# Modulation weights in pieces of two K-tiles by 1024 columns, scale ahead of shift by halves, three input blocks begun on the first half of the K-tiles

## The reference, cut to what matters

```python
def ada_modulation(cvec, w_mod, b_mod):            # w_mod: 2048 x 12288
    m = jax.nn.silu(cvec) @ w_mod + b_mod
    return jnp.split(m[:, None, :], N_MOD, axis=-1)

sh1, sc1, g1, sh2, sc2, g2 = ada_modulation(cvec, lp['w_mod'], lp['b_mod'])
h = rmsnorm(x, lp['n1']) * (1.0 + sc1) + sh1
... = split_columns(h @ lp['w_in'])
```

## Time and profile before

| | |
|---|---|
| median of 3 runs | 2429.8 us (2429.21 to 2432.45) |
| profiled execution, its own time | 2430.1 us |
| its span in the trace | 2428.3 us |
| TensorE busy | 2204.9 us (91%) |
| first matmul with w_in | 144.92 us |
| first matmul behind the mixed stage (L711) | 642.54 us |
| `w_mod` loads | 96 of 1024 KB |

### The profile page before, as it was taken

The page is one execution under the profiler, slowest core; times in us unless marked ns, Lnnn a source line. Parts: engine busy times, 40 slices in busy tenths (PEclk is TensorE's granted clock), DMA queues, the critical chain, the costliest instruction groups (busy, mean ns, idle before and its releaser), DMA issues.

```text
span 2428.3 us, 44041 instructions
## 1 busy us (share of the span) xinstructions
PE 2204.9 (91%) x19325; PEld 1948.0 (80%) x19325; DVE 1142.7 (47%) x2079; ACT 773.5 (32%) x1300; POOL 94.9 (4%) x140
## 2 busy tenths in 40 slices
PE   3789999999777888886997999999999999999997
PEld 1268888888545666665997999999999999887885
DVE  1122223544495787874346444444444444445445
ACT  2122222222253434342334332333333333333432
POOL 1000000000301111110000000000000000000000
PEclk8579999999876999998998999999999999999998
DMA  8977777777701001004325334334334435333341
GB/s 293 348 254 233 231 225 243 245 224 226 179 2 28 7 3 33 3 5 171 109 87 174 122 128 133 122 123 137 122 122 132 129 122 180 132 122 121 121 133 59
DMA packets 283472, 338.78 MB, mean 140 GB/s; under 512 B 9502, under 2 KB 268180, under 8 KB 281425
## 3 DMA queue, kind: packets, MB, share of 16 engines
q1 hardware_dynamic: 281440, 329.77, 42.2%
q0 software_dynamic: 1840, 6.20, 1.0%
HBM read 328.43 MB, written 10.28 MB: 139 GB/s over the span
## 4 chain that ended last, share of the span: by engine, by line
PE 80%; DVE 11%; DMA 4%; ACT 2%; issue 2%; POOL 0%; DVEq 0%; SPq 0%; POOLq 0%; ACTq 0%
PE ps L616 23%; PE ps L618 22%; PE ps L617 22%; DMA ring<-in_w_mod_dram 3%; PE ps L654 3%; PE ps L663 1%; PE ps L808 1%; PE ps L802 1%; PE ps L798 1%; DVE arena L1681 1%; PE ps L979 1%; DMA arena<-in_x_sample_dram 1%; DVE stat L1542 1%; DVE w_split L1386 1%; PE ps L818 1%
## 5 line engine op out<-in xcount | busy, mean ns | idle before, releaser
L1386 DVE TENSOR_TENSOR w_split<-ring,w_split 128x1024 fp32r<-128x1024 f32 (+1 forms) x392 | 475.7, 1219 | 760.2 <-ACT w_split L1086 759.9
L1086 ACT ACTIVATE w_split<-ring 128x1024 fp32r<-128x1024 f32 (+1 forms) x392 | 407.4, 1052 | 736.1 <-PE ps L618 592.1
L616 PE MATMUL ps<-h_split,w_split 128*128 128x384 f32 x1776 | 598.2, 337 | 11.8 <-DVE w_split L1386 8.5
L618 PE MATMUL ps<-h_split,w_split 128*128 128x384 f32 x1776 | 594.9, 335 | 0.0
L617 PE MATMUL ps<-h_split,w_split 128*128 128x384 f32 x1776 | 594.9, 335 | 0.0
L616 PEld LDWEIGHTS ps<-h_split,w_split 128*128 128x128 f32 x1776 | 334.7, 188 | 23.8 <-issue 12.0
L617 PEld LDWEIGHTS ps<-h_split,w_split 128*128 128x128 f32 x1776 | 334.6, 188 | 0.0
L618 PEld LDWEIGHTS ps<-h_split,w_split 128*128 128x128 f32 x1776 | 334.5, 188 | 0.0
L616 PE MATMUL ps<-w_split,h_split 128*128 128x256 f32 x960 | 275.2, 287 | 12.6 <-DVE w_split L1386 12.6
L617 PE MATMUL ps<-w_split,h_split 128*128 128x256 f32 x960 | 272.2, 284 | 0.0
L618 PE MATMUL ps<-w_split,h_split 128*128 128x256 f32 x960 | 272.1, 283 | 0.0
(11 more groups left out here) (362 smaller groups left out, 2732.4 us busy)
## 6 DMA issues: line engine op xcount, KB each, us to landing
ring<-in_w_mod_dram SPq DMA_DIRECT2D x96, 1024.0 KB, 8.2
ring<-in_w_up_dram SPq DMA_DIRECT2D x88, 1024.0 KB, 5.1
ring<-in_w_in_dram SPq DMA_DIRECT2D x46, 1024.0 KB, 6.9
ring<-in_w_down_dram SPq DMA_DIRECT2D x44, 1024.0 KB, 5.3
ring<-in_w_out_dram SPq DMA_DIRECT2D x16, 1024.0 KB, 5.8
arena<-in_x_sample_dram SPq DMA_DIRECT2D x4, 1024.0 KB, 12.8
x_mid<-arena SPq DMA_DIRECT2D x1, 3072.0 KB, 10.2
h_f<-x_mid SPq DMA_DIRECT2D x1, 3072.0 KB, 9.9
```

What stands on the lines that cost most here:

```text
L616: mm(o_, lh, rh, start=start, stop=False)
L618: return mm(o_, ll, rh, start=False, stop=stop)
L1086: AC(wh[k % SPLITS][:, 0:width(n)], arrived(n), ACT.Copy).then_inc(s_hi, 1)
L1386: V.tensor_tensor(wl[k % SPLITS][:, 0:w], arrived(n), wh[k % SPLITS][:, 0:w].bitcast(F32), ALU.subtract).then_inc(s_lo, 1)
```

## The change

`w_mod` comes in pieces of two K-tiles by 1024 columns (rows of 4 KB); a block is 1024 columns, so there are 12 blocks of 8 pieces and not 48 of two. A part is one K-tile; its four matmuls of 256 columns have the same stationary tile and go to the four groups of PSUM rows, which now hold four groups of columns; `mod_cols` spreads them with eight columns of the identity. The order is scale of K-tiles 0 to 7, shift of K-tiles 0 to 7, scale and shift of 8 to 15. Three pieces of `w_in` (the first half of the K-tiles of its blocks 0, 1 and 2) are moved into the second half of the front: the stream begins with 21 modulation pieces (0 to 20), then w_in (21), six modulation pieces, w_in (28), five modulation pieces, w_in (34), w_in block 0's second half (35), and 64 modulation and 44 more w_in pieces mixed. x is loaded after the first four pieces. The transposes of x move behind part 21 (the end of piece 10), the sigmoid of c ahead of the squares, and one tensor_reduce for expb goes. `h_mod` multiplies a half of the K-tiles at once; the shift is added in `h_hi` (four activations for a pair, in place of one) and `h_lo` (four in place of one).

```diff
@@ -59,7 +59,11 @@
-N_MOD = 6 * D // BLK
+MG = 4
+MOD_W = MG * BLK
+MOD_KP = PIECE // MOD_W
+MP = KT // MOD_KP
+N_MOD = 6 * D // MOD_W
...
@@ -69,27 +73,30 @@
-N_EARLY = 2 * D // BLK
-MOD_ORDER = [8 * (i % 2) + i // 2 for i in range(N_EARLY)] + list(range(N_EARLY, N_MOD))
-MIXED = [("mod", N_EARLY, 0), ("mod", N_EARLY, 1)]
-_left = [("mod", i, p) for i in range(N_EARLY + 1, N_MOD) for p in range(2)]
-_in = [("in", j, p) for j in range(len(IN_BLOCKS)) for p in range(2)]
+N_EARLY = 2 * D // MOD_W
+MOD_ORDER = [2, 0, 3, 1] + list(range(N_EARLY, N_MOD))
+EARLY_IN = 3
+STREAM = [("mod", i, p) for i in range(2) for p in range(MP)]
+for _p in range(2 * MP):
+    STREAM.append(("mod", 2 + _p // MP, _p % MP))
+    if _p in (4, 10, 15):
+        STREAM.append(("in", (4, 10, 15).index(_p), 0))
+_left = [("mod", i, p) for i in range(N_EARLY, N_MOD) for p in range(MP)]
+_in = [("in", j, 1) for j in range(EARLY_IN)] + [("in", j, p) for j in range(EARLY_IN, len(IN_BLOCKS)) for p in range(2)]
 for _i, _piece in enumerate(_in):
-    MIXED.append(_piece)
-    MIXED += _left[_i * len(_left) // len(_in):(_i + 1) * len(_left) // len(_in)]
-STREAM = [("mod", i, p) for i in range(N_EARLY) for p in range(2)] + MIXED
+    STREAM.append(_piece)
+    STREAM += _left[_i * len(_left) // len(_in):(_i + 1) * len(_left) // len(_in)]
...
@@ -106,12 +113,9 @@
+FRONT = MOD_END[3] + SPLITS
+H_AT = {MOD_END[1] + SPLITS - 1: (0, 1, 2, 3)}
+H_AT.update((MOD_END[3] + k, (4 + k,)) for k in range(4))
...
@@ -435,11 +443,13 @@
-            for t, src in ((0, a["x_prompt"][0]), (1, a["x_sample"][0, 0:P]), (2, a["x_sample"][0, P:2 * P])):
-                sp.dma_start(x[:, t, :], src).then_inc(s_x, 16)
             for n, (kind, i, p) in enumerate(STREAM):
+                if n == RING:
+                    for t, src in ((0, a["x_prompt"][0]), (1, a["x_sample"][0, 0:P]), (2, a["x_sample"][0, P:2 * P])):
+                        sp.dma_start(x[:, t, :], src).then_inc(s_x, 16)
                 if kind == "mod":
-                    load_piece(n, a["w_mod"][0], BLK * MOD_ORDER[i], BLK, p)
+                    src = a["w_mod"][0][MOD_KP * P * p:MOD_KP * P * (p + 1), MOD_W * MOD_ORDER[i]:MOD_W * (MOD_ORDER[i] + 1)]
+                    load(n, src.rearrange("(k p) c -> p k c", p=P), MOD_KP)
...
@@ -640,27 +650,21 @@
             def mod_part(n, i, p):
-                if n % 2 == 0 and p == 0 and i >= 2:
-                    if i - 2 < N_EARLY:
-                        pe.wait_ge(s_mrow, i - 1)
-                    else:
-                        pe.wait_ge(s_mcol, i - 1)
+                q = MOD_KP * p + n % 2
+                if q == 0 and i >= 2:
+                    pe.wait_ge(s_mcol, i - 1)
                 pe.wait_ge(s_w[n // 2 % RING], 16 * (n // 2 // RING + 1))
-                w_raw = arrived(n).rearrange("p (k c) -> p k c", k=KQ)
-                for k in range(KQ):
-                    q = KP * p + KQ * (n % 2) + k
-                    last = mm(ps[32 * k:32 * k + 2, i % 2, 0:BLK], c2_t[:, 2 * q:2 * q + 2], w_raw[:, k, :], start=(q == k), stop=(q == KT - KQ + k))
+                w_raw = arrived(n).rearrange("p (g c) -> p g c", g=MG)
+                for g in range(MG):
+                    last = mm(ps[32 * g:32 * g + 2, i % 2, 0:BLK], c2_t[:, 2 * q:2 * q + 2], w_raw[:, g, :], start=(q == 0), stop=(q == KT - 1))
                 last.then_inc(s_blk, 1)

             def mod_cols(i):
                 pe.wait_ge(s_mrow, i + 1)
...
                 for j in range(2):
-                    last = mm(ps[:, bank, at + 2 * j:at + 2 * j + 2], modrow[:, i % 2, toks(j)], expb[:, 9:11], start=True, stop=True)
+                    last = mm(ps[:, i % 2, BLK + 2 * MG * j:BLK + 2 * MG * (j + 1)], modrow(i)[:, toks(j)],
+                              ident.rearrange("p (g b) -> p g b", g=MG)[:, :, 0:2], start=True, stop=True)
...
@@ -699,7 +701,13 @@
-                if n - 3 in MOD_LAST:
+                if n == MOD_END[0] + 5:
+                    mod_cols(0)
+                    for t in range(3):
+                        turn_x(t)
+                if n in (MOD_END[1] - 1, MOD_END[2] + 1, MOD_END[3] - 1):
+                    mod_cols(1 + (n > MOD_END[1]) + (n > MOD_END[2] + 1))
+                if n - 3 in MOD_LAST and MOD_LAST[n - 3] >= N_EARLY:
                     mod_cols(MOD_LAST[n - 3])
...
@@ -1086,38 +1094,39 @@
+            def h_hi(j):
+                ac.wait_ge(s_mcol, 2 if j < PAIRS // 2 else 4)
+                ac.wait_ge(s_hm, j + 1)
+                for k in (2 * j, 2 * j + 1):
+                    for g, cols in ((0, slice(0, P)), (1, slice(P, TOK))):
+                        last = AC(hh[:, k, cols], xT[:, k, cols], ACT.Identity, bias=modcol[:, k, g:g + 1])
+                last.then_inc(s_hh, 1)
+
+            ac.wait_ge(s_vt, 1)
+            AC(csig, ps[:, 0, 0:2 * KT], ACT.Sigmoid).then_inc(s_csig, 1)
             for t in range(3):
                 ac.wait_ge(s_x, 48)
                 AC(junk, x[:, t, :], ACT.Square, accum_out=stat[:, t:t + 1]).then_inc(s_ssq, 1)
                 ac.wait_ge(s_ssq, t + 1)
-            ac.wait_ge(s_vt, 1)
-            AC(csig, ps[:, 0, 0:2 * KT], ACT.Sigmoid).then_inc(s_csig, 1)
+            mod_row(0)
...
-                AC(hh[:, 2 * j:2 * j + 2, :], xT[:, 2 * j:2 * j + 2, :], ACT.Copy).then_inc(s_hh, 1)
...
@@ -1419,45 +1427,58 @@
+            def h_mod(half_):
+                ks = slice(KT // 2 * half_, KT // 2 * (half_ + 1))
+                dv.wait_ge(s_mcol, 2 * half_ + 1)
+                link(V.scalar_tensor_tensor(scol[:, ks, :], modcol[:, KT:2 * KT, :][:, ks, :], 1.0, n1[:, ks, :], ALU.add, ALU.mult))
+                dv.wait_ge(s_xc, 12)
+                for k in range(ks.start, ks.stop):
+                    for g, cols in ((0, slice(0, P)), (1, slice(P, TOK))):
+                        last = V.tensor_scalar(xT[:, k, cols], xT[:, k, cols], scol[:, k, g:g + 1], None, ALU.mult)
...
+            def h_lo(j):
+                dv.wait_ge(s_mcol, 2 if j < PAIRS // 2 else 4)
+                dv.wait_ge(s_hm, j + 1)
+                dv.wait_ge(s_hh, j + 1)
                 for k in (2 * j, 2 * j + 1):
...
+                    for g, cols in ((0, slice(0, P)), (1, slice(P, TOK))):
+                        last = V.scalar_tensor_tensor(hl[:, k, cols], xT[:, k, cols], modcol[:, k, g:g + 1],
+                                                      hh[:, k, cols].bitcast(F32), ALU.add, ALU.subtract)
+                last.then_inc(s_h, 1)
...
+            for n in range(FRONT):
+                if n == MOD_END[0]:
+                    mod_col(0)
+                    h_mod(0)
+                if n == MOD_END[1]:
+                    mod_col(1)
+                if n == MOD_END[2] + 2:
+                    mod_col(2)
+                    h_mod(1)
+                if n == MOD_END[3]:
+                    mod_col(3)
...
```

More of the change, by code:

```diff
@@ L86 @@
 DOWN_W = PIECE // DOWN_KT
-MOD_LAST = {2 * n + 1: i for n, (kind, i, p) in enumerate(STREAM) if kind == "mod" and p == 1}
+MOD_LAST = {2 * n + 1: i for n, (kind, i, p) in enumerate(STREAM) if kind == "mod" and p == MP - 1}
 IN_LAST = {2 * n + 1: i for n, (kind, i, p) in enumerate(STREAM) if kind == "in" and p == 1}
@@ L91 @@
 MOD_END = {i: n + 1 for n, i in MOD_LAST.items()}
-PAIRS = N_EARLY // 2
+PAIRS = KT // 2
 SPLIT = [n for n in range(P_OUT) if STREAM[n // 2][0] == "in"]
@@ L258, in build @@
         crstd, o = carve(arena, o, CW)
-        modrow, _ = carve(arena, o, 2, BLK)
+        modrow2, _ = carve(arena, o, 2, BLK)
+        modrow1, _ = carve(ubuf, 0, 2, BLK)
         knew, o = carve(arena, o, 768)
@@ L413, in used, with modrow @@
                 eng.wait_ge(s_kd, n - P_DOWN + 1)
+        def modrow(i):
+            return (modrow1 if i < N_EARLY else modrow2)[:, i % 2, :]
         block = ctx.enter_context(nc.Block())
@@ L630, in _, with turn_x @@
                 tr(ps[:, g, 0:rows], vrow[0:rows, g, :], ident[0:rows, 0:rows]).then_inc(s_vt, 1)
-            for t in range(3):
+            def turn_x(t):
                 pe.wait_ge(s_xn, t + 1)
@@ L658, in mod_cols @@
                 pe.wait_ge(s_mrow, i + 1)
-                if i >= 2:
-                    pe.wait_ge(s_mcol, i - 1)
-                bank, at = (2 + i % 2, 0) if i < N_EARLY else (i % 2, BLK)
                 for j in range(2):
-                    last = mm(ps[:, bank, at + 2 * j:at + 2 * j + 2], modrow[:, i % 2, toks(j)], expb[:, 9:11], start=True, stop=True)
+                    last = mm(ps[:, i % 2, BLK + 2 * MG * j:BLK + 2 * MG * (j + 1)], modrow(i)[:, toks(j)],
+                              ident.rearrange("p (g b) -> p g b", g=MG)[:, :, 0:2], start=True, stop=True)
                 last.then_inc(s_mcT, 1)
@@ L670, in in_part @@
                 if n % 2 == 0 and p == 0:
-                    if j == 0:
-                        pe.wait_ge(s_mcol, N_EARLY)
                     for s in range(tiles):
@@ L1086, in hi, with mod_row @@
                 AC(wh[k % SPLITS][:, 0:width(n)], arrived(n), ACT.Copy).then_inc(s_hi, 1)
```

(48 more changed lines are left out.)

1 line of the change is left out of this document (removed).

## The result

The changed kernel takes 2392.85 us (median of 4 runs, 2391.87 to 2393.49) against 2431.03 for the kernel before beside it; the ratio is 0.9842 (95% interval 0.9829 to 0.9854). The profiled execution took 2392.75 us, its span is 2390.9. The forecast was 2389.

What follows compares the result with a forecast made beforehand. DMA engines were taken to bound the front until 144.92 us, PE the mixed stage after it. Front 13.8 us gained and mixed stage -26.8, together -40.6 on 2430.1, gave 2389 us; range 2373 to 2408.

Steps and rivals of the forecast that it cites:

- Start: Front: PE enters the modulation parts at about 20 us, 17 earlier, while the DMA doesn't stop.
- Rate: Front: 4 KB rows at 410 GB/s, 2.56 us a modulation piece; 28 pieces after x save 12.6 us.
- first rival: Front: 4 KB rows bring nothing, rate stays 348 GB/s, pieces take 3.01 us; 2397 us in all; chance 0.22.
- 372 GB/s: Front: estimate from the skill's fixed 3 cycles per packet, 2.82 us a modulation piece, about 2393 us in all.
- The transposes: Front: 48 transposes of x behind piece 10 keep PE longer than the ring lasts; 4.8 us lost.
- 8 us for the table: Front: the padded bias table, 2.7 MB within the DRAM, costs 8 us at 348 GB/s, as before.
- The w_in pieces: Front: early w_in pieces 21 and 28 hold PE longer than the ring lasts; 5.8 us lost, twice.
- second rival: Front: clock stays at half through the early w_in pieces, each stall grows by 6.5 us; 2408 us; chance 0.12.
- the third: Front: no stalls, hidden by pieces left in the ring and a clock already up; 2373 us; chance 0.10.
- Mixed stage: PE-bound stage: two w_in halves fewer -16.6, two modulation pieces more +1.8, fewer mod_cols -12.0; sum -26.8 us.
- slower rival: Modulation parts: four matmuls with one stationary tile take turns, up to +175 us in the mixed stage, some 2565; chance 0.04.
- The sum: Front 13.8 us gained and mixed stage -26.8, together -40.6 on 2430.1; what comes later only shifts.

Runs made afterwards that it cites:

- run 4: Changed kernel with the start as it was: x loaded ahead of the ring, squares ahead of the sigmoid, transposes ahead of the parts; 2402.21 us (0.9877).
- runs 1 and 2: Changed kernel with each modulation piece in two loads of one K-tile, landing as 1 KB rows (2410.24 us) or, as control, 4 KB rows (2396.69 us).
- Run 6: Changed kernel with the bias table's 2.7 MB copy held back until 80 parts are done, out of the front; 2392.36 us (0.9835).
- run 5: Changed kernel with the second part of w_in pieces 21 and 28 moved, on PE, behind the next two modulation pieces; 2388.08 us (0.9820).
- run 8: Changed kernel with the two mod_cols matmuls issued four times over for the mixed stage's 8 modulation blocks; 2403.00 us (0.9878).
- Runs 3 and 8: The first is the changed kernel without the three early w_in pieces in the front, 2388.68 us (0.9823); the second is run 8.

## Why the prediction was right

- *Start.* PE began at 16.94, not 20: the small vectors landed 2 us earlier, and the sigmoid began 0.3 us behind the first of their transposes and not behind them all. It changed nothing, since the next piece had to land first, at 28.96, 2.3 us later than my 26.6. The first 10 us moved 287 GB/s on average where I had 406 from 2 us on; that is 0.4 MB, 1 us. The rest of the delay isn't traced. Undone in run 4: 8.5 us, with the order of the loads, the sigmoid and the place of the transposes changed together.
- *Rate.* 2.56 us a piece and 407 GB/s: the full microsecond of a lone w_down piece was the right row, and runs 1 and 2 show the length of the rows, as packets, as the cause. The first rival (348 stays) is out. So are the 372 GB/s that the prediction estimated from the Trainium skill (DMA: Bandwidth & Descriptors, "Why small descriptors are slow (HBM only)"): the steady front has 407.
- *The transposes.* The step that was wrong in itself: 4.8 us of stall and 8 us for the table were added, but both fell on the same time. From 45.43 (piece 10) to 66.35 (piece 15) five pieces took 20.9, which is 12.8 + 8.1. Run 6 takes the table away and leaves a stall of 3.7 there, so 4.8 was also somewhat too much. Against it piece 10 came 3.4 us late (45.43, forecast 42). That piece 21's matmuls began at 84.50 against a forecast of 85 is two errors that cancel, which is luck.
- *The w_in pieces.* Distances of 25.2 and 22.0 between the three, forecast 24 and 22; run 5 shows PE's block as the cause of at least half of each stall. The clock was up again after 5.6, 4.3 and 2.7 us of dense matmuls, not 4 each time: the second rival (half clock throughout) is out, and the third (no stalls) too.
- *Mixed stage.* 470.9 against a forecast of 470.8, again by two errors that cancel. PE's idle time, which I left alone, rose from 8.8 to 12.8 us, and as much more than forecast went from its busy time. Counted from start to start, mod_cols by themselves gave the 12.0 of the forecast. But the modulation's matmuls took 0.5 less, where two more pieces were to cost 1.8: a mod_cols between two parts makes them take 2 x 0.54 = 1.08 in place of 0.98, as the rows under run 8 show, and 19 fewer such places give 1.9 of these 2.3 us. The w_in matmuls took 18.3 less and not 16.6, in part since their clock came up after 2.7 us and not 4. Runs 3 and 8 agree with the sum of the terms, not with each of them.
- *Four matmuls with one stationary tile.* They overlap as before: the four pieces used at 95.59 (32 matmuls, 64 records) took 3.63 us, 0.45 for each of eight parts. The slower rival is out.
- *The sum.* -40.0 up to L719 against -40.6. Of the 3 us between 2389 and 2392, 2.6 are the part behind, which differs by 7 us between profiles of kernels that don't differ there and goes with the time at the half clock. The rate, PE's blocks and the mod_cols left out were forecast rightly as mechanisms; that the whole came out to 0.2% owes something to the two cancellations.

## What to carry to other kernels

Where a ring of slots feeds an engine that works in order, a step is free only while it is shorter than the loads that stand behind it; a longer one stops the DMA engines while the engine itself is fully busy, and cutting it up on that engine gets part of the time back (here half). In a stage that the DMA engines bound, look first at the length of the rows that a load moves in one stretch, on the side where they leave and on the side where they land. What is moved out of such a stage must be cut small, or it takes back in the next one much of what it gave. And a stage that comes out as forecast isn't yet forecast rightly: its terms have to be held against the trace one by one.

## What was not expected of the hardware

Loads with rows of 1 KB end at 348 to 349 GB/s at a DMA share of 1.09, with rows of 4 KB at 400 to 412 at 1.02 to 1.04, in the front of one core, and 349 against 400 between two kernels that differ only in how a row lands (4 KB in HBM in both). A copy of 2.7 MB within the DRAM took 8 us from the ring's loads in the front and made PE stand for 5 of 20 us in a stage whose mean DMA share was 0.68; in eight pieces it cost nothing that these runs can tell.
